# A hybrid encoder step on one core: attention heads taken in pairs, and the gated-linear-attention level products made in place inside the attention loop

## The reference

```
h = xn @ w_in;  qa, ka, va, qb, kb, vb, gb, lr = split(h)     # qa, ka normed per head
A:  p = softmax(qa ka^T / 8 + bias);   oa = p va               # also returned: ka, va
B:  b = cumsum(log_sigmoid(lr @ gate_w + gate_b) / 16)
    attn[i,j] = sum_d q[i,d] k[j,d] exp(b[i,d] - b[j,d])   (j <= i)
    o = attn v + (q exp(b)) S;   S' = exp(b_last) S + (k exp(b_last - b))^T v
y = concat(oa, rms_norm(ob) * silu(gb)) @ w_out
```

## Time and profile before

| | us |
|---|---|
| median of 3 runs | 1464.96 (1463.9 to 1465.55) |
| the profiled execution | 1469.65 |
| its span in the profile | 1467.9 |
| PE busy | 1416.7 (97%) |
| DVE busy | 744.1 (51%) |
| ACT busy | 503.4 (34%) |
| POOL busy | 80.1 (5%) |
| chain that ended last | PE 86%, DVE 8%, ACT 4%, rest 2% |

### The profile page before, as it was taken

How to read it: one execution, slowest core, us unless ns; L and a number is a source line. 1 busy time by engine, 2 the same in 40 slices (tenths; PEclk the granted TensorE clock), 3 DMA queues, 4 the chain that set the end, 5 groups by cost and what they waited for, 6 DMA issues and landing times.

```text
span 1467.9 us, 25862 instructions
## 1 busy us (share of the span) xinstructions
PE 1416.7 (97%) x10648; PEld 1346.8 (92%) x10648; DVE 744.1 (51%) x1037; ACT 503.4 (34%) x824; POOL 80.1 (5%) x107
## 2 busy tenths in 40 slices
PE   6999999699999999999999999997999999999998
PEld 5999777576999999999999899995999999999998
DVE  6693543776454433434333888996454433434322
ACT  4323443533333312213222553445443312213212
POOL 5101001100200000000002000000200000000000
PEclk9999999788999999999999999999999999999999
DMA  5423200121223222232322111100223222222321
GB/s 161 148 87 101 74 16 15 61 89 36 86 87 87 86 87 86 89 88 82 105 73 82 58 33 55 57 29 7 87 87 87 86 86 87 88 88 82 104 76 54
DMA packets 104651, 112.94 MB, mean 77 GB/s; under 512 B 3343, under 2 KB 102266, under 8 KB 104315
## 3 DMA queue, kind: packets, MB, share of 16 engines
q1 hardware_dynamic: 102459, 101.43, 21.9%
q0 software_dynamic: 2048, 10.36, 2.0%
q10 hardware_dynamic: 64, 0.02, 0.0%
HBM read 104.58 MB, written 7.21 MB: 76 GB/s over the span
## 4 chain that ended last, share of the span: by engine, by line
PE 86%; DVE 8%; ACT 4%; issue 1%; DMA 1%; POOL 0%; SPq 0%; ACTq 0%; DVEq 0%; POOLq 0%
PE ps L942 68%; PE ps L1237 4%; PE ps L1039 3%; PE ps L1081 2%; PE ps L927 2%; PE ps L1053 2%; DVE rstd L1419 1%; ACT w_h L539 1%; DVE w_l L1330 1%; PE ps L1068 1%; PE ps L1145 1%; ACT xn L864 1%; DVE pair L1587 1%; DMA x_rows<-in_x_sample 1%; PE ps L1160 0%
## 5 line engine op out<-in xcount | busy, mean ns | idle before, releaser
L942 PE MATMUL ps<-x_h,w_h 128*128 128x272 f32 x1280 | 269.0, 291 | 10.1 <-DVE x_l L1359 7.2
L1330 DVE TENSOR_TENSOR w_l<-w_raw,w_h 128x2048 fp32r<-128x2048 f32 x92 | 211.8, 2302 | 107.6 <-ACT w_h L539 107.5
L942 PE MATMUL ps<-x_l,w_h 128*128 128x272 f32 x1280 | 265.6, 289 | 0.0
L942 PE MATMUL ps<-x_h,w_l 128*128 128x272 f32 x1280 | 264.6, 288 | 0.0
L539 ACT ACTIVATE w_h<-w_raw 128x2048 fp32r<-128x2048 f32 x92 | 175.3, 1906 | 238.8 <-PE ps L942 238.8
L942 PEld LDWEIGHTS ps<-x_h,w_h 128*128 128x128 f32 x1280 | 201.7, 189 | 15.1 <-DVE x_l L1359 9.4
L942 PE MATMUL ps<-xf_l,w_h 128*128 128x272 f32 x1024 | 212.7, 288 | 0.0
L942 PE MATMUL ps<-xf_h,w_h 128*128 128x272 f32 x1024 | 212.0, 288 | 0.0
L942 PE MATMUL ps<-xf_h,w_l 128*128 128x272 f32 x1024 | 211.5, 288 | 0.0
L942 PEld LDWEIGHTS ps<-x_h,w_l 128*128 128x128 f32 x1280 | 201.3, 189 | 0.0
L942 PEld LDWEIGHTS ps<-x_l,w_h 128*128 128x128 f32 x1280 | 200.9, 188 | 0.0
(11 more groups left out here) (249 smaller groups left out, 1736.4 us busy)
## 6 DMA issues: line engine op xcount, KB each, us to landing
w_raw<-in_w_ffn_up SPq DMA_DIRECT2D x32, 1024.0 KB, 5.5
w_raw<-in_w_ffn_down SPq DMA_DIRECT2D x32, 1024.0 KB, 4.8
w_raw<-in_w_in_ab SPq DMA_DIRECT2D x12, 1024.0 KB, 5.4
w_raw<-in_c_w_pw SPq DMA_DIRECT2D x12, 1024.0 KB, 5.2
w_raw<-in_w_out_ab SPq DMA_DIRECT2D x4, 1024.0 KB, 5.4
resid_scratch<-resid POOLq DMA_DIRECT2D x1, 2176.0 KB, 8.1
resid<-resid_scratch POOLq DMA_DIRECT2D x1, 2176.0 KB, 8.9
x_rows<-in_x_prompt SPq DMA_DIRECT2D x4, 512.0 KB, 5.7
```

The lines of the kernel that those rows point to most:

```text
L942: ins = pe.matmul(ps[:, 2 * m + t, 0:HALF], a[s][:, k, w], b[:, k, t * HALF:(t + 1) * HALF], start=(k == 0 and q == 0), stop=(k == KT - 1 ...
L1330: dve.tensor_tensor(w_l[s][:], w_raw[:, s], w_h[s][:].bitcast(F32), ALU.subtract).then_inc(w_lo, 1)
```

## The change

- The attention loop takes heads in pairs: 20 turns. A turn issues the two heads' scores one behind the other, on partitions 0 to 63 and 64 to 127, and the two heads' value products alternately, to output partitions 0 to 63 and 64 to 127; the loop runs `turn(2t-4)`, `scores(t)`, two projection steps, `turn(2t-3)`, the remaining one or two steps, `values(t-2)`. One ACT copy moves both heads' outputs.
- The level products of B are made in place: `lev` holds exp(..)k in the first half of each level's blocks and exp(..)q in the second; both come from one tile. Each `pairs` level becomes two matmuls over 64 partitions, one per head, into two PSUM banks. `lq0`, `lq1`, the other-head zeros and `copy_lone_q` go; the factor 1/8 of q moves into its evacuation.
- `kd`, `qe` and all level differences, exponentials and products move from behind the loop into its turns 5 to 21, on DVE and ACT.
- K's rows are turned and copied before the loop, in `gates`, and stored before it, since they now lie over the probabilities: DVE waits for that store before the first turn. B's value rows are turned in the last two turns.
- `pick_pairs` works in two halves, not three banks; `outputs(d)` does both heads kind by kind. Unit 12 of the weights is split after the last `pairs`, since the levels of the second group lie over its slot. SP's wait before unit 12 stands at the same point under a new count.

```diff
-    lq0 = sb(ctx, "lq0", [P, 2 * KT * 256])[:, 0:7 * TOK].rearrange("p (l b t) -> p l b t", l=7, b=2)
+    lev0 = sb(ctx, "lev0", [P, 2 * KT * 256])[:, 0:7 * TOK].rearrange("p (l t) -> p l t", l=7)
...
-    lev = sb(ctx, "lev", [P, 2, 2 * KT * 256])[:, :, 0:7 * TOK].rearrange("p n (l t) -> p n l t", l=7)
+    lev1 = sb(ctx, "lev1", [P, 2, 2 * KT * 256])[:, 0, 0:7 * TOK].rearrange("p (l t) -> p l t", l=7)
...
+    kd, qe = sq[:, :, 0:TOK], xn[:, 1:3, :]
+    prob, prob_T = probs[:, 0:4, :], probs[:, 4:6, :]
+
+
+    ck_rows, k_rows = bias[:, 2:4, :], probs[:, 0:TT + 1, :]
...
+    TURNS = 5 * HA // 2
+    def head(n):
+        return n // 10 * 2 + n % 2
+    def block_of(n):
+        return n // 2 % 5
...
+    G_K, G_CK, G_VB, G_END = 5, 10, 12, 17
...
-    split_turns = (1, 11, 21)
+    LEVELS = ((0, 1), (2, 3), (4, 5, 6))
+    split_turns = (0, 5, 10)
...
-        sp.wait_ge(pairs_done, 15)
+        sp.wait_ge(pairs_done, 10)
...
+        pool.wait_ge(rows_out[0], 5)
+        pool.wait_ge(rows_out[1], 5)
+        store_rows(k_rows, ak_prompt, ak_sample)
...
-        pool.wait_ge(w_lo, 12)
-        other_head_zero(0)
-
-        pool.wait_ge(o_copied, 5 * HA)
-        pool.wait_ge(bias_ready, HA)
-        other_head_zero(1)
-        pool.wait_ge(stored, 16 * 2)
+
+        pool.wait_ge(o_copied, TURNS)
+        pool.wait_ge(stored, 16 * 4)
         pool.dma_start(spare, resid_dram).then_inc(resid_back, 16)
-        pool.wait_ge(rows_out[0], 14)
-        store_rows(k_rows, ak_prompt, ak_sample)
-        pool.wait_ge(stored, 16 * 4)
...
+        copy_rows(6)
+        copy_rows(8)
...
+        for t in range(TURNS + 3):
+            if t >= 3:
+                copy_o(t - 3)
+            for e in range(2):
+                if 1 <= t <= TURNS:
+                    exp_scores(2 * t - 2 + e)
+                if 2 <= t <= TURNS + 1:
+                    copy_probT(2 * t - 4 + e)
             if t in split_turns:
                 split_hi(0, 0, U_ATT + 1 + split_turns.index(t))
-            if t == 8:
+            if t == 6:
                 act.wait_ge(bt_ready, 10)
                 act.activation(eb, bt, ACT.Exp, scale=1.0 / 16).then_inc(eb_ready, 1)
-
-        copy_lone_q(0)
-        copy_rows(LATE)
-        copy_rows(LATE + 1)
-        for n in range(2):
-            act.wait_ge(kd_diff, n + 1)
-            act.activation(kd[:, n, :], kd[:, n, :], ACT.Exp, scale=1.0 / 16).then_inc(kd_exp, 1)
-        for l in range(7):
-            cols = slice(0, SEQ if l < 2 else TOK)
-            act.wait_ge(lev_diff, 2 * (l + 1))
-            act.activation(lev[:, :, l, cols], lev[:, :, l, cols], ACT.Exp, scale=1.0 / 16).then_inc(lev_exp, 1)
-            for g in (LATE + 2 + l, LATE + 9):
-                if g < LATE + 9 or l == 6:
+            if t == 7:
+                for g in range(2):
+                    act.wait_ge(kd_diff, g + 1)
+                    act.activation(kd[:, g, :], kd[:, g, :], ACT.Exp, scale=1.0 / 16).then_inc(kd_exp, 1)
+            if 13 <= t < 16:
+                exp_level(0, t - 13)
+            if 17 <= t < 20:
+                exp_level(1, t - 17)
+            if t == TURNS:
+                copy_rows(G_VB)
+                copy_rows(G_VB + 1)
+            if t == TURNS + 1:
+                for g in range(G_VB + 2, G_END):
                     copy_rows(g)
...
+        act.wait_ge(pairs_done, 20)
+        split_hi(U_OUT, 0, 0)
...
         def gates():
+            pe.wait_ge(qk_norm, 10)
+            early_rows(G_K)
             pe.wait_ge(lr_ready, 1)
-            pe.wait_ge(rows_out[0], 3)
-            pe.wait_ge(rows_out[1], 2)
+            pe.wait_ge(rows_out[0], 5)
...
+        def scores(t):
+            hp, c = t // 5, t % 5
+            M = width(c)
+            parts = ((k_tiles(hp), 0, keys(2 * t)),) if c < TT else (
+                (ck_T[:, hp, :], 0, PAST), (proj[:, T_K + hp, SEQ:TOK], PAST, DEC))
+            for k, at, nk in parts:
+                for e in range(2):
+                    n, rows = 2 * t + e, slice(e * DA, (e + 1) * DA)
+                    if at == 0 and n >= 2:
+                        pe.wait_ge(score_read, n - 1)
+                    ins = pe.matmul(ps[0:M, 4 + e, at:at + nk], proj[rows, T_Q + hp, frames_back(c)],
+                                    k[rows, 0:nk], start=True, stop=True)
+                    if at + nk == keys(n):
+                        ins.then_inc(score_done, 1)
...
+                for e in range(2):
+                    h = 2 * hp + e
+                    ins = pe.matmul(ps[e * DA:(e + 1) * DA, 7, 0:M], rows[:, h * DA:(h + 1) * DA],
+                                    prob_T[0:w, e, j * M:(j + 1) * M], start=(j == 0), stop=(j == len(tiles) - 1))
...
+        for t in range(TURNS + 2):
+            steps = list(range(64 * t // TURNS, 64 * (t + 1) // TURNS)) if t < TURNS else []
+            if t >= 2:
+                turn(2 * t - 4)
+                if t == TURNS:
+                    pe.wait_ge(slot_free[0], tile0(U_OUT) // 2)
+                    turn_rows(G_VB)
+            if t < TURNS:
                 scores(t)
+            for j in steps[:2]:
                 project_step(j)
+            if t >= 2:
+                turn(2 * t - 3)
+            for j in steps[2:]:
+                project_step(j)
+            if t == TURNS:
+                turn_rows(G_VB + 1)
+            elif t > TURNS:
+                pe.wait_ge(slot_free[1], tile0(U_OUT) // 2)
+                turn_rows(G_VB + 2)
+                turn_rows(G_VB + 3)
+                pe.wait_ge(rows_out[0], 7)
+                turn_rows(G_VB + 4)
+            if t >= 2:
+                values(t - 2)
...
+        def pairs(d):
+            g, c = d // 5, d % 5
+            M = width(c)
+            if c == 0:
+                pe.wait_ge(lev_ready[g], 1)
+            for half in range(2):
+                if d:
+                    pe.wait_ge(picked, 2 * d - 1 + half)
+                for n in range(4 * half + (0 if c < TT or half else 2), 4 * half + 4):
+                    for b in range(2):
+                        rows = slice(b * DKB, (b + 1) * DKB)
+                        out = ps[0:M, 2 * half + b, n % 4 * P:n % 4 * P + M]
+                        if n == 7:
+                            l, q = proj[rows, T_KB + g, frames(c)], proj[rows, T_QB + g, frames(c)]
+                        else:
+                            w = levels()[n]
+                            l = lev[g][rows, n, frames(c)]
+                            q, out = (a.rearrange("p (a h c) -> p a h c", h=2, c=w)[:, :, 1, :] for a in (l, out))
+                        ins = pe.matmul(out, l, q, start=True, stop=True)
+                ins.then_inc(pairs_done, 1)
+        def outputs(d):
+            c = d % 5
+            M = width(c)
+            for m in (2 * d, 2 * d + 1):
+                h, b = head_of(m)[0], m % 2 * DKB
+                if m >= 2:
+                    pe.wait_ge(state_ready, m - 1)
+                pe.matmul(ps[b:b + DKB, 6 + m % 2, 0:DVB], kd_rows[0:M, c, h * DKB:(h + 1) * DKB],
+                          vb_rows[0:M, c, h * DVB:(h + 1) * DVB], start=True, stop=True).then_inc(kv_done, 1)
+            pe.wait_ge(picked, 2 * d + 2)
+            for m in (2 * d, 2 * d + 1):
+                h = head_of(m)[0]
+                if m >= 2:
+                    pe.wait_ge(ob_ready, m - 1)
+                ins = pe.matmul(ps[:, 4 + m % 2, 0:M], vb_rows[0:M, c, h * DVB:(h + 1) * DVB],
+                                pair[0:M, d % 2, m % 2, 0:M], start=True, stop=(c == 0))
+                if c == 0:
+                    ins.then_inc(ob_done, 1)
+            if c:
+                st = state if c < TT else state_s
+                for m in (2 * d, 2 * d + 1):
+                    h, b = head_of(m)[0], m % 2 * DKB
+                    pe.matmul(ps[:, 4 + m % 2, 0:M], st[b:b + DKB, h // 2, :], qe[b:b + DKB, h // 2, frames(c)],
+                              start=False, stop=True).then_inc(ob_done, 1)
+        pe.wait_ge(rows_out[0], 11)
+        pairs(0)
...
+            if u == 6:
+                dve.scalar_tensor_tensor(out=halves(out), in0=slot(m), scalar=DKB ** -0.5, in1=halves(r_tok),
+                                         op0=ALU.mult, op1=ALU.mult).then_inc(slot_free[m], 1)
+                return
...
+        def level_products(g, group):
+            dve.wait_ge(lev_exp, 3 * g + group + 1)
+            for l in LEVELS[group]:
+                z, _, k, q = by_halves(g, l)
+                dve.tensor_tensor(z[:, :, 0, :], z[:, :, 0, :], k[:, :, 0, :], ALU.mult)
+                ins = dve.tensor_tensor(z[:, :, 1, :], z[:, :, 1, :], q[:, :, 1, :], ALU.mult)
+            if group == 2:
+                ins.then_inc(lev_ready[g], 1)
...
+        dve.wait_ge(stored, 16 * 4)
+        for t in range(TURNS + 2):
+            for e in range(2):
+                if 1 <= t <= TURNS:
+                    inverse_sum(2 * t - 2 + e)
+                if t < TURNS:
+                    biased(2 * t + e)
```

(69 more changed lines are left out.)

312 lines of the change are left out of this document (95 added, 217 removed).

## The result

The changed kernel takes 1427.99 us, the median of 4 executions (1425.54 to 1431.18); the kernel before, run beside it, 1465.26. The ratio is 0.9746, with a 95% interval of 0.9721 to 0.9772. The forecast was 1430 in a range of 1413 to 1449. The profiled execution took 1426.12 us with a span of 1424.4; that of the kernel before took 1469.65. So the two profiled executions lie 43.5 us apart, where the medians lie 37.3 apart.

A forecast was written before the change was run, and what follows sets the result against it. PE was taken to bound the attention loop, level work the stretch behind it. Terms +4.4 - 14.5 (loop) - 17.5 (behind it) - 8 (linear attention) + 1 = -34.6 gave 1435.0 profiled, 1430 us for the median, range 1413 to 1449.

The forecast's parts named there:

- K rows and the store: In `gates` and before the first scores: K's rows cost 4.1 us, DVE's wait for their store 0.3; together +4.4.
- Scores: Attention loop: neighbouring scores of two heads on different partitions overlap in part, saving 5.2 + 3.8 = 9 us.
- three slots of four: Loop scores: one head's second half runs with the other's first, saving 1.3 us a pair beside the fixed part.
- Values: Attention loop: value products alternating between two heads overlap and save fixed parts, 11.6 us; bounds 2.8 and 13.5.
- 2J+1 slots: Loop values: J key tiles for two alternating heads cost 2J+1 slots, not 4J, saving 2.2 us a pair.
- An extra change of shape: Attention loop: a turn goes from values to transposes to scores, one change more at 0.17 us each; costs 3.4 us.
- DVE's stall: Attention loop, turns 12 to 19: added level work makes DVE late and PE's transposes wait; 2.5 us, bounds 0 and 10.
- Behind the loop: Last projection step to first pick: 13.6 of 31.2 us remain, saving 17.5; bounds 12 and 20.
- Linear attention: Linear-attention loop: full steps at 4.4 us, short ones at 2.3, 3 us of waits; 43 against 51, saving 8.
- The end: After the last pairs: unit 12's split makes the reciprocal start 1 us later; +1, bounds 0 to 4.
- all-overlap rival: Both loops: all neighbours on different partitions overlap; -47.6 us, 1417; chance 0.10.
- drain rival: Both loops: each alternation of partitions drains PE, 300 x 0.17 = 51 us against 16 saved; +35, 1500; chance 0.08.

The follow-up runs named there:

- warm kernel: Also called the warm run: changed kernel with SiLU early, 20 small matmuls before the kd-rows wait, 14, 6, 14, 6 before pairs of steps 3, 4, 8, 9; 1419.41 us.
- warm kernels: Changed kernel, SiLU early, 20 small matmuls before the kd-rows wait, more before steps 2 to 9: 6 to 14, 1418.03 us; 14 each, 1416.85; 60 full-width fillers, 1413.05.

## Why the prediction was right, and where it was not

The median came within 2 us of the forecast, but two large terms were wrong and cancelled in part: the loop gave 13.9 us more than forecast, linear attention 9.1 less. The mechanism named (PE-bound loop, overlap of the halves, level work under PE) is shown; the sum was partly luck. For the profiled executions, in which its terms were worked out, the forecast was 1435.0 and the result 1426.1, 8.9 off; the median hides this, as the profiled execution of before stood 4.4 above its median and that of after 1.9 below.

- **K rows and the store: +4.4; measured +4.6.** DVE did wait for the store, 1.8 us, ahead of the first scores' maximum, to 155.05, just past the 155 that was to make this part wrong; but PE was not held behind it, and the whole +4.6 was there when PE began the scores. The forecast had taken the clock as 1.00: where it fell behind the new waits in `gates`, this part cost up to 7.3 us (156.1 against 148.8), so the agreement is luck of the execution.
- **Scores: -9; measured -14.0.** The failed step is "matmuls start in program order: A's second half and B's first run together, three slots of four". The five blocks of both heads take 0.42, 0.63, 0.85, 1.06 and 0.61 us, 3.57 a pair against 2 x 3.53: all of one head vanishes, and three slots of four become two.
- **Values: -11.6; measured -13.1.** The failed step is "2J+1 slots". 0.37, 0.59, 0.81, 1.03 and 0.59 us are 3.39 a pair, against 2 x 3.33: 2J slots. The bound of 13.5, both heads' instructions wholly side by side, was the truth.
- **An extra change of shape: +3.4; measured -0.8 at most.** Scores and values save 3.49 + 3.27 = 6.76 of the 6.95 us a pair, so nothing was added. The failed step is "one change of shape more": in the rows two heads' turns of before change shape six times (scores to projection, projection to values, values to scores, twice), a turn of after four times. The two that went are the two fixed parts that were already counted as saved; none came in addition.
- **DVE's stall: +2.5; measured 0.** DVE is at 9.35 of 9.35 us in the last turns, as forecast, and PE waits nowhere. DVE's lateness was in the slack of the pipeline of two turns.
- **Behind the loop: -17.5; measured -18.5.** 13.6 us were forecast to remain, 12.8 did; 251.30 to 253.29 for the first pairs instead of 2.7 is most of the difference.
- **Linear attention: -8; measured +1.1.** The failed step is "I take 4.4" for a step, with "a low clock at the short steps" inside 3 us of waits: it was priced at the full clock but for those. Pairs are 1.99 us where the clock is full: loads of 64 partitions on two halves do run together (28 of them cover 1.6 us), while a single one still takes 187 ns. So the earlier trace rows were read rightly, a half-height load is no cheaper, and used wrongly: they say nothing on two at once. But the gap that lost the clock sits ahead of the whole loop, not at the short steps, and light steps did not bring the clock back. The prediction named a granted clock of 0.5 within the loop as what would break it as a whole; it came in this loop, and the scores' and values' surplus covered it. A full step is 6.08 us (262.32 to 268.40) where the step before had 4.5; in the warm kernel it is 3.42. With the clock held, the picks take 33.5 us against 44.6 before: -11, within the forecast's bounds and on the side of full overlap. The saving of 4 that the prediction gives for pairs of 3.4 us is a slip, since 8 x 5.1 + 2 x 2.3 + 3 = 48.4 leaves 2.6; the sum did not use it.
- **The end: +1; measured +0.9.** It lies on the chain as said, but moving it off gained nothing at the end (15.43 us for 15.52).

The all-overlap rival (0.10) had the mechanism, and its 1417 would have needed the clock; the warm kernels, at 1413 to 1418, are that rival. The drain rival is out: 12 alternations inside the scores and 26 inside the values cost nothing that a row shows. The Trainium skill ("TensorEngine Tiling (Array Packing)", Key Properties) says that different tiles execute loads and matmuls in parallel; the trace agrees, to the full factor of two, for row halves (scores, pairs) and column halves (values) alike. I had given that rule less weight than a slot count of my own. For the clock, the Trainium skill ("TensorE: Matmul & The Clock Gate", Part 1) advises that PE should have no long idle gaps. The trace agrees in part only: the first fall came with a gap, of 2.22 us, but the fall in the warm run had no gap in the rows for 15 us before it.

## What to carry to other kernels

Two half-array matmuls on disjoint halves cost what one costs, if they alternate or come in short runs of one shape; put something between them and the price of the second is back in full. Price a stage that becomes shorter at both clock levels: the slower version here lost the clock and got it back inside the stage, and the changed one, once it had lost it, did not for 50 us. In such a stage any gap ahead of it or in it decides for all that follows. Before filling gaps, look at the granted clock by windows of a few microseconds, and at where PE is idle: fillers with the earlier SiLU gained 15 us in the changed kernel, while in the kernel before, where most of them stood at no gap, they lost 4.

## What the runs showed of the hardware

- The granted clock stayed at 0.50 for 50 us in which PE's rows show 50.3 of 52.1 us busy; in the warm run it fell with PE busy 3.00 of 3.00 us before and after. Busy time in the rows does not tell whether the clock holds. In the kernel before it came back at 322, in pairs over 128 partitions. The half-array pairs, at twice the pace, are what sets the changed stage apart; that they are the cause is an inference, since nothing here varied them alone.
- 20 bf16 matmuls of 64 weight columns and 256 moving ones (2.37 us) ahead of a wait carried the clock across it; 4 a step did not carry it over the SiLU, and 6 to 14 a step, with the SiLU moved, held it for the whole loop (34.9 us at 1.00). Whether the SiLU had to move for that was not tried.
- The clock can fall or hold in the same code: behind waits of 0.54, 0.35 and 0.86 us in `gates` it fell in 9 of 12 profiled executions.
- Blocks of 4 instructions a head on column halves overlap as well as alternating ones (0.59 us for both), blocks of 8 only by half (1.51 us, against 1.03 alternating and 2.04 one after the other). Six a head with a change of shape between the heads do not overlap (1.15 against 0.59).
